# A hybrid decoder step on one core: the attention probabilities turned and multiplied later in each projection step, and two low-part subtractions moved off the first gather of the experts

## The chip, the cores and the metric

The kernel runs on one NeuronCore of a Trainium2 chip. The time is the device time of one execution in microseconds (us), and of several executions the median. The engines are TensorE (PE in the profile, with the loading of weights as PEld), VectorE (DVE), ScalarE (ACT), GpSimd (POOL) and SyncE (SP, which here only issues transfers). They run their own instruction streams and wait for each other through semaphores.

## The reference

One inference step of a decoder with one layer, for 1024 prompt tokens and 8 sample tokens, model width 1024:

```
h   = rmsnorm(x, n1) * (1 + sc1) + sh1
rq, rk, rv, rg, sq, sk, sv, za, zb = split(h @ w_in)
retention (4 heads of 128, chunks of 128, decay per head) on rotated rq, rk and on rv
sliding-window attention (8 query heads of 64 on 2 key heads, window 128, a learned sink per head)
    s = q k^T / 8 in the band;  m = max(max s, sink);  p = exp(s - m) / (sum exp(s - m) + exp(sink - m));  o = p v
merged = sigmoid(za) * (o_ret * silu(rg) @ w_up_ret) + sigmoid(zb) * (o_swa @ w_up_swa)
x   = x + g1 * (merged @ w_o)
h2  = rmsnorm(x, n2) * (1 + sc2) + sh2
experts: best group of 4, best 2 of its 8 experts, w2(silu(h2 w1) * (h2 w3)) weighted
y   = rmsnorm(x + g2 * experts, final_g)
```

The factors sh, sc and g come from silu(c) @ w_ada + b_ada, with w_ada of 1024 x 6144. Everything is in float32. Large products are done in three passes with each factor split into a high part (rounded to the matmul's float32r) and a low part (the rest): hi*hi + hi*lo + lo*hi.

## The kernel before

The tokens are 8 tiles of 128 prompt tokens and one of 8 sample tokens. The program is written out by hand, one stream for each engine, and the order of each stream is that in which its calls stand in the code. A step that stands earlier in one stream runs only when its semaphores allow, and holds all behind it.

**Projection steps.** `STEPS` has 36 entries (h, t): for each of four heads, tiles 0 to 8 (8 is the sample tile). The pass m of the loop (m from 0 to 36) works on three of them at once, PE in this order: parts 0 and 1 of the projection of `STEPS[m]` (`project_h`, L1700, 12 products of 512 columns), the turning of the rotated q and k of step m-1 (`turn_qk`, L1742), the turning of the probabilities of step m-2 into bank p5 (`turn_probs`, L1767), part 2, the product of the turned probabilities with V (`window`, L1778, into columns 256 to 383 of bank p7), the scores of step m-1 (L1747, L1751), part 3, and the output products of step m-1 (`outputs`, L1759 to L1761, into columns 0 to 255 of p7). In eight of the passes (`ADA_AT`: two per head) PE also does one part of the later modulation in bank p6 (`ada_later`, L1805), between the turning of the probabilities and part 2.

DVE goes, in pass m, through the rotation for step m-1 (L1099 to L1157), the normalising of the probabilities of step m-2 (L1187 to L1189), the copy out of the window's product (`window_out`, L1200), the softmax preparation of step m-1 (`weigh`, L1171 to L1183), in the eight passes the addition of the bias to the modulation (L1233, signals mod_r), and the copies out of p7 (`retention_out`, L1194 and L1195, signals st_u). ACT copies v and a scaled k, then the turned q and k (L770), then the turned probabilities (`probs_out`, L781, signals pT_e), squares the outputs (L785) and does the exponentials of step m-1 (L775). In the pass in which PE projects a sample tile, ACT also rounds the next head's weights in four parts (`head_round`, L738) and DVE subtracts to get their low parts (`head_rest`, L1088); parts 1 to 3 of the rounding stand behind the copy of the probabilities. Behind t = 2 of the later heads DVE normalises the outputs of the head before.

**From routing to the experts.** Behind the output projection each tile gets its second norm (DVE L1393, L1394), is turned and copied (ACT L899), gets router logits (PE L1977, DVE L1398), and DVE works out the expert and place of each token. When DVE has written the slots (L1508, L1509), POOL gathers the rows of the first three experts' tokens from DRAM (`gather_block`, L648), PE turns them (L2032), ACT and DVE split them, and PE multiplies them with the first expert's weights. These are split as well: ACT rounds each half (`half13`, L926 for the first expert, L941 later; each signals w13_hi) and DVE subtracts (`rest13`, L1512, in place, 128 x 2048; each signals w13_lo). For the first expert ACT's two halves stand behind the copy of the last tile, and DVE's two subtractions between the slots for the gather and those for the scatter.

## Time and profile before

| | us |
|---|---|
| median of 3 runs | 1367.56 |
| lowest and highest | 1364.56, 1368.78 |
| profiled execution | 1362.71 |
| its span, first to last instruction | 1360.9 |
| PE busy | 1223.7 (90%) |
| DVE busy | 747.4 (55%) |
| ACT busy | 509.0 (37%) |
| POOL busy | 172.8 (13%) |
| mean granted clock of PE, share of full speed | 0.959 |

The span is cut into stages by what PE does: first norm and keys and values to 98 us, projection steps to 442, gates and merge to 816, output projection and routing to 968, experts from 977 to 1304, and the weighted sum with the final norm to the end. Matmuls are pipelined, and one that starts behind a busy PE is shown from the point at which it begins to run to its modelled end, so two neighbours may overlap; the distance from one start to the next is then the better measure. A row that says xN stands for N instructions in a row. A number in brackets at a row's end is the time for which the engine had nothing to do ahead of it, and what ended it; "issue" there is time for which the profile shows no reason.

### The profile page before, as it was taken

To read this page: it belongs to the slowest core of one execution; us is meant where nothing else is said; L and a number is where in the kernel's file an instruction comes from. 1 tells how busy PE (TensorE), PEld (TensorE's weight loads), DVE (VectorE), ACT (ScalarE), POOL (GpSimd) and SP (SyncE) were. 2 spreads that over 40 slices of the span, in tenths; PEclk is the share of its full clock that TensorE was granted. 3 is DMA by queue.
4 is the path that set the end of the run, shared out by engine and by line. 5 is a ranking of instruction groups with operands and counts; after the bars stand their busy time and mean duration, and the time that the engine had idled before them with its cause. 6 is when DMAs were issued, how large, how long until landed. Compare 5 with 4: busy or idle time off the path is not lost.

```text
span 1360.9 us, 18012 instructions
## 1 busy us (share of the span) xinstructions
PE 1223.7 (90%) x6849; PEld 937.9 (69%) x6849; DVE 747.4 (55%) x1437; ACT 509.0 (37%) x862; POOL 172.8 (13%) x169
## 2 busy tenths in 40 slices
PE   4789999999998999999999998998499999988966
PEld 1677667667675788888888886886367666666732
DVE  0766565656566443111222206447599888887937
ACT  1643323323333221100111103111288878777832
POOL 2110000000000000000000001110222354444101
PEclk8799999999999999999999998999599999999988
DMA  9533222322222032111111005234589999999754
GB/s 359 196 141 111 89 80 88 131 101 80 88 83 82 28 123 114 47 47 47 47 46 44 2 0 188 78 136 179 182 299 371 373 353 367 358 354 357 291 222 179
DMA packets 40718, 219.75 MB, mean 161 GB/s; under 512 B 7432, under 2 KB 15056, under 8 KB 27978
## 3 DMA queue, kind: packets, MB, share of 16 engines
q1 hardware_dynamic: 32194, 197.15, 38.8%
q0 software_dynamic: 7536, 18.51, 4.0%
q10 hardware_dynamic: 928, 3.28, 0.7%
q8 instruction: 38, 0.62, 0.2%
q14 instruction: 22, 0.18, 0.0%
HBM read 202.03 MB, written 24.72 MB: 167 GB/s over the span
## 4 chain that ended last, share of the span: by engine, by line
PE 64%; DVE 16%; DMA 12%; issue 3%; ACT 3%; SPq 0%; POOL 0%; POOLq 0%; DVEq 0%; ACTq 0%
PE p L1934 10%; PE p L2042 8%; DMA G<-in_we 8%; PE p L1700 8%; PE p L1938 6%; PE psS L1961 4%; PE p L1870 3%; PE psS L1934 3%; PE p L1961 3%; PE psS L2061 3%; PE psS L1938 2%; PE p L1778 1%; DVE work L1189 1%; PE p L1767 1%; PE psS L1751 1%
## 5 line engine op out<-in xcount | busy, mean ns | idle before, releaser
L1700 PE MATMUL p<-A 128*128 128x512 f32 (+3 forms) x1080 | 259.0, 387 | 9.8 <-DVE A L1082 9.8
L1700 PEld LDWEIGHTS p<-A 128*128 128x128 f32 (+1 forms) x1080 | 175.7, 184 | 61.7 <-issue 12.7
L2042 PE MATMUL p<-C 128*96 128x512 f32 x768 | 194.0, 404 | 21.0 <-DVE C L1587 21.0
L2042 PEld LDWEIGHTS p<-C 128*96 128x96 f32 x768 | 122.0, 165 | 78.2 <-issue 31.1
L1512 DVE TENSOR_TENSOR C<-G,C 128x2048 fp32r<-128x2048 f32 x64 | 146.2, 2286 | 35.5 <-ACT C L941 35.5
L1341 DVE TENSOR_TENSOR work<-p,work 128x384 f32<-128x384 f32 (+1 forms) x36 | 18.6, 516 | 238.0 <-ACT work L871 237.6
L1934 PE MATMUL p<-A,B 128*128 128x384 f32 (+1 forms) x864 | 142.7, 323 | 2.0 <-DVE M L1274 2.0
L1934 PEld LDWEIGHTS p<-A,B 128*128 128x128 f32 x864 | 136.9, 188 | 4.5 <-issue 2.2
L941 ACT CAST C<-G 128x2048 fp32r<-128x2048 f32 x62 | 118.8, 1916 | 26.0 <-DMA G<-in_we 21.2
L2061 PE MATMUL psS<-C 128*96 128x512 f32 x384 | 95.9, 398 | 1.9 <-DVE C L1599 1.9
L655 POOL DMA_INDIRECT y_dram<-M,slotY x32 | 76.4, 2388 | 106.2 <-ACT M L975 106.2
L1938 PE MATMUL p<-M 128*128 128x384 f32 (+1 forms) x288 | 87.2, 452 | 0.0
L775 ACT ACTIVATE work<-work,small 128x256 f32<-128x256 f32 x64 | 32.1, 503 | 136.3 <-DVE small L1183 135.7
L2061 PEld LDWEIGHTS psS<-C 128*96 128x96 f32 x384 | 59.6, 162 | 24.7 <-DVE C L1581 2.1
L1576 DVE TENSOR_TENSOR C<-G,C 128x2048 fp32r<-128x2048 f32 x31 | 70.9, 2288 | 9.0 <-ACT C L947 8.8
L1938 PEld LDWEIGHTS p<-M 128*128 128x128 f32 x288 | 53.8, 190 | 23.9
L871 ACT ACTIVATE work<-p 128x384 f32<-128x384 f32 (+1 forms) x36 | 15.1, 455 | 133.4 <-PE psS L1938 133.4
L1961 PE MATMUL psS<-B 128*128 128x512 f32 (+1 forms) x240 | 59.5, 405 | 5.4 <-DVE B L1371 5.4
L648 POOL DMA_INDIRECT M<-h_dram,slotT x32 | 47.2, 1475 | 127.6 <-PE p L2032 106.7
L1200 DVE COPY M<-p 128x128 f32<-128x128 f32 x32 | 9.3, 291 | 96.1 <-PE p L1778 96.1
L947 ACT CAST C<-G 128x2048 fp32r<-128x2048 f32 x31 | 59.3, 1914 | 0.0
L626 POOL CAST B<-F 128x1024 fp32r (+2 forms) x8 | 8.9, 1112 | 396.5 <-DVE F L1347 331.1
(284 smaller groups left out, 1811.7 us busy)
## 6 DMA issues: line engine op xcount, KB each, us to landing
G<-in_we SPq DMA_DIRECT2D x32, 2048.0 KB, 18.0
G<-in_we SPq DMA_DIRECT2D x32, 1024.0 KB, 18.9
M<-in_w_ada SPq DMA_DIRECT2D x8, 2048.0 KB, 8.0
M<-in_x SPq DMA_DIRECT2D x18, 512.0 KB, 4.7
M<-in_rope SPq DMA_DIRECT2D x45, 192.0 KB, 2.4
D<-in_w_qkv SPq DMA_DIRECT2D x4, 2048.0 KB, 8.9
F<-in_lift SPq DMA_DIRECT2D x8, 1024.0 KB, 5.0
M<-y_dram SPq DMA_DIRECT2D x8, 1024.0 KB, 11.9
```

The lines of the kernel that those rows point to most:

```text
L648: pool.indirect_dma_start(out=xg[0:CAP, slot], out_offset=None, in_=h2_dram, in_offset=bass.IndirectOffsetOnAxis(ap=slotT[:, b:b + 1], axi ...
L655: pool.indirect_dma_start(out=y_dram, in_=yb[0:CAP, slot], in_offset=None, out_offset=bass.IndirectOffsetOnAxis(ap=slotY[:, b:b + 1], axis=0),
L941: nc.scalar.copy(half(h13, u), half(we[slot], u)).then_inc(s["w13_hi"], 1)
L947: nc.scalar.copy(h2w, we[slot][:, 4096:6144]).then_inc(s["w2_hi"], 1)
L1512: nc.vector.tensor_tensor(half(we_lo[slot], u), half(we[slot], u), half(h13, u), ALU.subtract).then_inc(s["w13_lo"], 1)
L1576: nc.vector.tensor_tensor(we_lo[slot][:, 4096:6144], we[slot][:, 4096:6144], h2w, ALU.subtract).then_inc(s["w2_lo"], 1)
L1700: last = mm(out, x[k][:, t0:t0 + rows], y(k), start=k == 0 and j == 0, stop=k == KD - 1 and j == 2)
L1934: mm(bs[j][:, 0:w0], w[slot][:, wc], x[:, cols], start=k == 0 and n == 0, stop=k == KD - 1 and n == 2)
L1938: last = mm(bs[2 + j][:, 0:w0], wy[slot][:, (4 * j + k) * P:(4 * j + k + 1) * P], src[:, k, cols], start=k == 0, stop=k == H - 1)
L1961: last = mm(o_bank[slot][n][0:rows], m[slot][:, k, 0:rows], w[k][:, cols], start=k == 0 and j == 0, stop=k == KD - 1 and j == 2)
L2042: last = mm(up_bank[slot][0:CAP, :], x[:, k, :], kcols(w, k), start=k == 0 and j == 0, stop=k == KD - 1 and j == 2)
L2061: last = mm(psS[0:CAP, nn, :], h[:, f, :], w[:, c0:c0 + 512], start=f == 0 and j == 0, stop=f == 1 and j == 2)
```

## The change

On PE, the turning of the probabilities moves from ahead of part 2 to behind it, and the product with V from ahead of the scores to behind part 3; its result goes into bank p6 and not p7. The modulation keeps its place ahead of part 2 and first waits for st_u of step m-2. As it uses p6 as well, in its passes PE waits for mod_r ahead of the product with V. On DVE, `window_out` moves behind `weigh` and the modulation's addition, and reads p6. ACT's order in the steps is as before.

At the experts' start, ACT's two roundings of the first expert's weights move ahead of the copy of the last tile; DVE's first subtraction moves ahead of the last tile's logits, and the second behind the slots for the scatter and the counts.

```diff
@@ ACT
+            half13(0)
+            half13(1)
             h2T_out(NT, NS)
             act.wait_ge(s["h2_r"], NT + 1)
             table(G2, 5, P)
-            half13(0)
-            half13(1)
@@ DVE, projection steps
-                nc.vector.tensor_copy(oswT[:, h, i * P:(i + 1) * P], p7[:, 256:384])
+                nc.vector.tensor_copy(oswT[:, h, i * P:(i + 1) * P], p6[:, 256:384])
...
-                    window_out(NT * h2 + t2_, h2, t2_)
                 if conv:
                     head_rest(conv, 1)
                 if t < NT:
                     weigh(n, h)
-                if conv:
-                    head_rest(conv, 2)
                 if m in ADA_AT:
...
+                if m >= 2 and STEPS[m - 2][1] < NT:
+                    window_out(NT * h2 + t2_, h2, t2_)
+                if conv:
+                    head_rest(conv, 2)
                 if t < NT:
                     retention_out(n, h, t)
@@ DVE, routing
             norm2(NT, NS)
+            rest13(0, 0, 0)
             logits(NT, NS)
...
-            rest13(0, 0, 0)
-            rest13(0, 1, 0)
             link(nc.vector.tensor_scalar(slot_y, s64[:, 0:NE], 2.0, float(2 * EMPTY), ALU.mult, ALU.add))
...
+            rest13(0, 1, 0)
+
             def expert(b, r):
@@ PE, window and projection steps
-                        last = mm(p7[r, 256:384], V_all[:, (i + b) * P + g * HD:(i + b) * P + (g + 1) * HD], prT[:, g, b, :],
+                        last = mm(p6[r, 256:384], V_all[:, (i + b) * P + g * HD:(i + b) * P + (g + 1) * HD], prT[:, g, b, :],
...
+                if m in ADA_AT:
+                    pe.wait_ge(s["st_u"], NT * prev2[0] + prev2[1] + 1)
+                    ada_later(ADA_AT[m])
+                if m < len(STEPS):
+                    project_h(m, 2)
                 if prev2:
...
                     turn_probs(NT * prev2[0] + prev2[1])
-                if m in ADA_AT:
-                    ada_later(ADA_AT[m])
-                if m < len(STEPS):
-                    project_h(m, 2)
-                if prev2:
-                    window(NT * prev2[0] + prev2[1], prev2[1])
                 if prev:
                     scores(NT * prev[0] + prev[1], prev[1])
                 if m < len(STEPS):
                     project_h(m, 3)
+                if m in ADA_AT:
+                    pe.wait_ge(s["mod_r"], ADA_AT[m] + 2)
+                if prev2:
+                    window(NT * prev2[0] + prev2[1], prev2[1])
                 if prev:
                     outputs(NT * prev[0] + prev[1], prev[0])
```

PE, the first pass with a part of the modulation (m = 2), before; L1805 is the modulation, L1767 the turning of the probabilities, L1778 their product with V:

```order
L1742 MATMUL p<-const,work 128x128 [waits rot]
L1742 MATMUL p<-const,work 128x128 x2
L1767 MATMUL p<-const,work 128x128 [waits pn_r,v_e,k_r]
L1767 MATMUL p<-const,work 128x128 x3
L1805 MATMUL p<-M,cT 32x128 [waits k_r,v_e,mod_r,ada_w]
L1805 MATMUL p<-M,cT 32x128 x31
L1700 MATMUL p<-A 128x512 x6
L1778 MATMUL p<-work,M 64x128 [waits v_e,st_u,pT_e]
L1778 MATMUL p<-work,M 64x128 x3
L1747 MATMUL p<-work 128x128 [waits qk_e]
```

And in the changed kernel, where the line numbers of this part are one higher (L1806, L1768, L1779):

```order
L1806 MATMUL p<-M,cT 32x128 [waits k_r,mod_r,v_e,ada_w,st_u]
L1806 MATMUL p<-M,cT 32x128 x31
L1701 MATMUL p<-A 128x512 x6
L1768 MATMUL p<-const,work 128x128 [waits pn_r,v_e,k_r]
L1768 MATMUL p<-const,work 128x128 x3
L1748 MATMUL p<-work 128x128 [waits qk_e]
L1752 MATMUL psS<-M,work 128x256 [waits kT_e]
L1752 MATMUL psS<-M,work 128x256
L1701 MATMUL p<-A 128x512 x6
L1779 MATMUL p<-work,M 64x128 [waits st_u,v_e,pT_e,mod_r]
L1779 MATMUL p<-work,M 64x128 x3
L1760 MATMUL p<-work 128x128 [waits at_r,kd_r,v_c]
```

The turning now has the six products of part 2 ahead of it, and the product with V the six of part 3 and, here, the wait for mod_r. In the other passes the same rows stand without the modulation and that wait.

DVE behind the slots for the gather, before; L1512 is the first expert's low parts, L1518 the slots for the scatter:

```order
L1509 TENSOR_SCALAR slotT<-work 96x29
L1512 TENSOR_TENSOR C<-G,C 128x2x1024 [waits w13_hi] x2
L1517 TENSOR_SCALAR work<-work 96x32
L1518 TENSOR_TENSOR slotY<-work 96x32 [waits dve_own]
L1521 COPY M<-p 128x32
```

And in the changed kernel, from the same instruction (L1515 there) to the first expert's tokens; the subtraction is L1476 there:

```order
L1515 TENSOR_SCALAR slotT<-work 96x29
L1516 TENSOR_SCALAR work<-work 96x32
L1517 TENSOR_TENSOR slotY<-work 96x32 [waits dve_own]
L1520 COPY M<-p 128x32
L1521 TENSOR_TENSOR work<-M,const 128x320 [waits dve_own]
L1523 TENSOR_REDUCE M<-work 128x32 [waits dve_own]
L1524 TENSOR_REDUCE M<-M 1x1 [waits dve_own]
L1525 CAST nover<-M 1x1 [waits dve_own]
L1476 TENSOR_TENSOR C<-G,C 128x2x1024 [waits w13_hi]
L1586 TENSOR_TENSOR C<-p,C 128x384 [waits xhi_r] x2
```

One of the two subtractions has gone up, ahead of the last logits, and the other stands behind seven small instructions.

## Rows read from the trace of the kernel before

**Rows 1.** PE's waits by cause: total us, times, longest, in the projection steps' lines.
```profile
PE p L1767 <- DVE work L1189: 10.3, 29, 2.7
...
PE p L1778 <- ACT work L781: 7.3, 4, 2.5
```
**Rows 2.** Timeline, a plain step on PE: start us, us, engine, line, count.
```profile
203.78 0.49 PE L1742 MATMUL p<-const,work 128*128 128x128 f32 x3
...
204.52 0.42 PEld L1767 LDWEIGHTS p<-const,work 128*128 128x128 f32 x4 [0.49 <-DVE work L1189]
204.52 0.66 PE L1767 MATMUL p<-const,work 128*128 128x128 f32 x4 [0.25 <-DVE work L1189]
...
204.93 1.64 PE L1700 MATMUL p<-A 128*128 128x512 f32 x6
...
206.50 0.66 PE L1778 MATMUL p<-work,M 128*64 128x128 f32 x8
...
207.09 0.49 PE L1747 MATMUL p<-work 128*128 128x128 f32 x2
...
208.15 1.65 PE L1700 MATMUL p<-A 128*128 128x512 f32 x6
...
209.63 0.38 PE L1759 MATMUL p<-work 128*128 128x128 f32 x2
```
**Rows 3.** Timeline, a step that turns no probabilities, on PE.
```profile
184.78 0.49 PE L1742 MATMUL p<-const,work 128*128 128x128 f32 x3
...
185.03 1.64 PE L1700 MATMUL p<-A 128*128 128x512 f32 x6
```
**Rows 4.** Timeline, a step with a part of the modulation, PE and DVE.
```profile
198.85 1.65 PE L1700 MATMUL p<-A 128*128 128x512 f32 x6
...
200.34 0.38 PE L1759 MATMUL p<-work 128*128 128x128 f32 x2
...
201.02 0.28 DVE L1233 TENSOR_TENSOR M<-p,M 128x128 f32<-128x128 f32 x1
```
**Rows 5.** Timeline, the two steps at the change from head 0.
```profile
168.43 1.05 ACT L738 CAST A<-D 128x1024 fp32r<-128x1024 f32 x1
...
170.16 1.21 DVE L1088 TENSOR_TENSOR A<-D,A 128x1024 fp32r<-128x1024 f32 x1
...
172.65 0.46 PE L1759 MATMUL p<-work 128*128 128x128 f32 x2 [0.21 <-DVE work L1176]
...
179.92 0.66 PE L1778 MATMUL p<-work,M 128*64 128x128 f32 x8 [1.59 <-ACT work L781]
```
**Rows 6.** Timeline, from the slots to the first gathered rows.
```profile
968.52 4.48 DVE L1512 TENSOR_TENSOR C<-G,C 128x2048 fp32r<-128x2048 f32 x2
...
969.53 4.51 POOL L648 DMA_INDIRECT M<-h_dram,slotT  x1 [20.26 <-DVE slotT L1509]
...
977.65 1.54 PE L2032 MATMUL p<-const,M 96*128 96x96 f32 x8 [9.58 <-DMA M<-h_dram,slotT]
```
**Rows 7.** Timeline, the last tile's logits, ACT and DVE.
```profile
952.93 0.19 ACT L899 COPY M<-p 128x32 f32<-128x32 f32 x1 [4.79 <-PE p L1970]
...
953.33 3.70 ACT L926 CAST C<-G 128x2048 fp32r<-128x2048 f32 x2
954.42 0.18 DVE L1398 TENSOR_TENSOR work<-p,brow 8x36 f32<-8x36 f32 x1 [2.60 <-PE p L1977]
```
**Rows 8.** Timeline, two later gathers and the subtractions beside them.
```profile
1006.73 2.28 DVE L1512 TENSOR_TENSOR C<-G,C 128x2048 fp32r<-128x2048 f32 x1
...
1008.58 1.29 POOL L648 DMA_INDIRECT M<-h_dram,slotT  x1 [4.12 <-PE p L2032]
...
1194.66 0.97 POOL L648 DMA_INDIRECT M<-h_dram,slotT  x1 [4.09 <-PE p L2032]
...
1195.01 2.29 DVE L1512 TENSOR_TENSOR C<-G,C 128x2048 fp32r<-128x2048 f32 x1 [2.27 <-ACT C L941]
```
**Rows 9.** Busy us (instructions), granted clock, DMA share, GB/s, end of the projection steps.
```profile
433.00:447.00 14.00, 8.53 (x43) 6.75 (x42) 11.48 (x37) 3.48 (x11) 1.86 (x2) 0.65 0.49 178
```

More of the change, by code:

```diff
@@ L919, in _ @@
             act.dma_start(FG, A["fg"].to_broadcast([P, D])).then_inc(s["tab_in"], 16)
-            h2T_out(NT, NS)
-            act.wait_ge(s["h2_r"], NT + 1)
-            table(G2, 5, P)
             def half13(u):
@@ L929, in _ @@
             half13(1)
+            h2T_out(NT, NS)
+            act.wait_ge(s["h2_r"], NT + 1)
+            table(G2, 5, P)
             act.wait_ge(s["gsh_r"], 3)
@@ L1472, in places, with rest13 @@
                     ALU.add, ALU.is_equal).then_inc(s["route_r"], 1)
+            def rest13(b, u, slot):
+                dve.wait_ge(s["w13_hi"], 2 * b + u + 1)
+                nc.vector.tensor_tensor(half(we_lo[slot], u), half(we[slot], u), half(h13, u), ALU.subtract
+                                        ).then_inc(s["w13_lo"], 1)
             merged_lo(NT, 0, NS)
@@ L1509, in _ @@
             nc.vector.tensor_scalar(slotT[:, 3:NE], s64[:, 3:NE], float(EMPTY), None, ALU.add).then_inc(s["route_r"], 1)
-            def rest13(b, u, slot):
-                dve.wait_ge(s["w13_hi"], 2 * b + u + 1)
-                nc.vector.tensor_tensor(half(we_lo[slot], u), half(we[slot], u), half(h13, u), ALU.subtract
-                                        ).then_inc(s["w13_lo"], 1)
-            rest13(0, 0, 0)
-            rest13(0, 1, 0)
             link(nc.vector.tensor_scalar(slot_y, s64[:, 0:NE], 2.0, float(2 * EMPTY), ALU.mult, ALU.add))
```

## The prediction

> **What bounds the kernel now.** I read the waits of TensorE (PE) first, then the timeline of one step of each kind, then the routing stretch, and last the POOL rows beside those of VectorE (DVE). The change touches two places that have nothing to do with each other.
>
> The first is the step phase, 98 to 442 us: 36 projection steps, four per eight token tiles and sample tile, and one closing pass. PE is the bound there. In the list of PE's waits [rows 1] stand 10.3 us in 29 waits for the turning of the probabilities (L1767, which waits for the normalising on DVE, L1189) and 7.3 us in 4 waits for their product with V (L1778, which waits for the copy on ScalarE, ACT, L781). In a plain step [rows 2] the reader sees that PE turns q and k at 203.78, can't go on, and starts L1767 at 204.52 with 0.25 us idle ahead; the third projection part comes at 204.93. In a step that turns no probabilities the third part follows 0.25 us behind the turning of q and k [rows 3]. Everything else in a plain step runs without a gap on PE. Rotation on DVE ends just as PE gets to the turning of q and k (behind a head's normalising it is late by 0.7 us), so that point has little slack; but it hangs on the output products, and what stands between these and the next turning is the same before and after.
>
> The second is the start of the experts. PE waits 9.58 us for the first gather [rows 6]. That gather takes POOL 4.51 us, where one that meets nothing takes 0.97 [rows 8], and DVE runs the two low-part subtractions of the first expert (L1512, 4.48 us) from just ahead of the first to its fourth microsecond.
>
> **The change, part by part.** *Plain steps.* Turning the probabilities moves behind the third part; the product with V moves from behind the third part to behind the fourth. Ahead of the third part go 204.93 - 203.78 = 1.15 us and 0.25 comes in their place: -0.90. Between the third part and the scores, L1767 now stands where L1778 stood; L1778 took 0.59 to the next instruction [rows 2], and L1767 with a waiting one behind it should take about as much; the third part before it may save some 0.05: call it -0.03. Behind the fourth part, 208.15 to 209.63 (1.48 us) becomes 1.57 (as 204.93 to 206.50) plus 0.59: +0.68. Sum -0.25 us a step, which is the idle time on L1767's row again. There are 4 such steps a head, 16 in all: -4.0. A few wait longer, 0.41 to 0.45, three of them right behind the normalising of a head's outputs: by the sum in [rows 1], 10.3 - 2.7 (the closing one) over 28 is 0.27 each, and the few over 0.25 make another -0.9, most of it where rotation was late too. Bounds per step: nothing (an issue gap of weight loads takes the stall's place) and -0.49, if the weight load's own idle time were what counted and all of it went.
> What hides the moved waits: the normalising has the whole third part as cover (1.6 us), ACT's copy the scores and the fourth part (2.2 us against 0.6).
>
> *Steps with a part of the later modulation (ADA_AT, 8 of them).* The product with V now writes the bank that these steps use, so PE waits ahead of it for mod_r, which DVE's addition L1233 gives. DVE does that addition behind the softmax preparation, as before. In [rows 4] the fourth part starts at 198.85 and L1233 ends at 201.30, so the product can start at about 201.35: 2.50 us behind the start of the fourth part, not 1.57. With 0.60 behind it and 1.49 saved (198.85 to 200.34) that is +1.61 instead of +0.68; against it stand the 0.90 ahead of the third part and a few hundredths. About +0.65 a step, 8 steps: +5.2. Bounds: +0.3 (the addition slips ahead of its row) and +0.95 a step (nothing won in exchange). Behind the waiting product stand the three output products and the next step's projection, so nothing covers it. This wait takes back what the plain steps give.
>
> *Steps at the change of heads.* ACT's copy of the probabilities stands ahead of its rounding of the next head's weights, part 1 (L738). That copy can't start now until PE has gone through the third part and the turning, so L738 begins some 1.05 us later than 168.43, DVE's L1088 (170.16 before, held there by the old copy of the window) about 0.4 later, and with it the scores' mask and the output products, which came at 172.65 [rows 5]. Here the product with V is already behind PE, so the 0.4 is all that is lost. In the next step PE does the whole third and fourth part before it needs ACT's copy; before, it stood 1.59 us [rows 5]. ACT's copy, which ended just ahead of 179.92, comes 0.6 later (the 0.4, and 0.2 for the window's copy that now stands ahead on DVE), so the product starts near 180.55 and the next head's projection 0.6 behind it, at 181.15. Before, the fourth part, 1.5 us, still stood between: 179.92 + 0.60 + 1.5 = 182.0. That is -0.87 a head, three heads: -2.6. Bounds 0 and -1.6 a head. At the fourth there is no projection left to put between: the 0.6 us by which DVE is late there stays, +0.6.
>
> Step phase: -4.0 - 0.9 + 5.2 - 2.6 + 0.6 = -1.7 us.
>
> *Low parts off the first gather.* Where the gathers overlap a DVE subtraction with both inputs in SBUF, they end a fixed time behind it: the one of 1008.58 ends at 1009.87, and L1512 ended at 1009.01, 0.86 before [rows 8]. The first ends at 974.04, 1.04 behind L1512's end at 973.00 [rows 6]. The gather of 1194.66 got in 0.35 us ahead of an L1512 and took 0.97 [rows 8]. So a gather is held at its beginning only. In the changed kernel DVE does seven small instructions behind the slots (1.9 us) and only then the second subtraction; a gather that starts at 969.53 is long past its beginning. It should end near 970.5: -3.5 us. The second gather may now be held by that subtraction, which costs nothing, as PE turns its rows ten microseconds later. The first subtraction goes into DVE's gap of 2.60 us ahead of the last logits at 954.42, 2.29 us into it (1006.73 is one of its kind); the two roundings on ACT (3.70 us for both) move ahead of the copies of 952.93, into 4.79 us in which ACT had nothing [rows 7]: they end by 952.0. They cost nothing, with 0.3 and 0.9 us to spare; if the cover were gone, a few tenths. What follows the gather (turning, tokens, the first expert, and the weight transfers that its end releases) is a chain, so the gain is kept through the expert stage. Bounds: 0 and -4.2.
> The Trainium skill, SBUF — State Buffer, section Who interferes with whom, says that a tensor_tensor with both inputs in SBUF holds GpSimd only where that reads SBUF, and infers that writing descriptors is not held by it. By that inference the subtractions would not be the cause and the sum would lack its 3.5 us. The rows disagree, unless it is the reading of the slots that is held, which the held beginning would fit.
>
> Sum: -1.7 - 3.5 = -5.2 us. The profiled execution took 1362.71 us (span 1360.9 and 1.8 around it), so it would come to 1357.5; it is 4.85 us faster than the median of the runs. From the median: 1367.56 - 5.2, about 1362.4 us.
>
> **The rivals.** *A: the first gather is slow because it is the first.* For it: no other gather in the profile is the first, and the subtractions hide nothing else. Against it: its end hangs on L1512's end as that of 1008.58 does [rows 6, 8]. Then only -1.7 is left: 1365.9 us.
> *B: the weight loads' idle time counts.* L1767's weight load stands idle 0.49 us, the product 0.25 [rows 2]. If all 24 plain and modulation steps win 0.24 more, and the heads too, it is -5.2 - 6.7: 1355.7 us. Against it: the step without probabilities, put together from [rows 3], gives 9.06 us and not 8.8.
> *C: the new wait lowers PE's clock.* Behind the two long waits at 438 and 441 us, 2.7 and 2.5 us, the granted clock of the stretch is 0.65 on average, so it fell to 1.2 GHz [rows 9]. If an idle 0.9 us in each of the eight steps did that too, at some 2 us a time, it would be +16 and the time 1378, slower. It decides from three such steps on. Against it: behind the 1.59 us of [rows 5] the eight products take the same 0.66 us as in a plain step.
>
> **How the numbers follow.** The main case 0.55, A 0.18, B 0.13, C 0.05; 0.09 is left for smaller mixtures, such as an expert stage that gives some of the gather's 3.5 us back to its weight transfers. The range: 1356.5 (most of B) to 1368 (A with modulation steps at their upper bound, +2.4, and little from the heads). A change over 0.3%, 4.1 us, is about what a measurement of this kernel can tell. The main case's 5.2 us is beyond it only by 1.1, so of its 0.55 some 0.40 counts as faster and 0.15 as the same. With B 0.13 and 0.03 of the rest: faster 0.56. A, 0.15 and most of the rest: same 0.37. C and a little: slower 0.07.
>
> **What would show it.** In the profile after: no PE wait on the turning of the probabilities but the closing one; 8 waits of 0.8 to 0.9 us on the product with V for the modulation's addition; the plain step 9.05 us from one turning to the next instead of 9.3; the step with modulation longer by 0.65; a first gather of about 1 us and the wait for it near 6 us. The prediction is wrong if the first gather stays at 4 us or more, if the plain steps shorten by 0.4, if the product's wait for mod_r isn't there, or if the expert stage from the first gathered rows to its end is longer than before by more than 2 us.

## The result and the profile after

| | before | after |
|---|---|---|
| median (runs), us | 1366.41 (4) | 1356.11 (4) |
| lowest and highest | 1364.56, 1368.78 | 1354.35, 1357.87 |
| profiled execution | 1362.71 | 1356.54 |
| its span | 1360.9 | 1354.6 |

The ratio of after to before over the runs is 0.9927, 95% interval 0.9909 to 0.9944. The medians differ by 10.3 us, where 5.2 were forecast, and 1356.11 lies just below the range, 1356.5 to 1368. In the two traces the span differs by 6.3 us. Cut into stages (start of the first turning of q and k, first gate product, start of the output projection, first gathered rows on PE, last expert, end) they show where it lies:

| stage, us | before | after | difference |
|---|---|---|---|
| to the first turning of q and k | 98.8 | 101.5 | +2.7 |
| projection steps | 343.9 | 337.1 | -6.8 |
| gates and merge | 378.9 | 379.3 | +0.4 |
| output projection, routing, first gather | 156.1 | 152.3 | -3.8 |
| experts | 337.0 | 338.0 | +1.0 |
| weighted sum and final norm | 46.2 | 46.4 | +0.2 |

The stages that the change touches, the second and the fourth, give -10.6. The first stage has no changed instruction and took between 97.9 and 102.2 us in the thirteen traces of this study; the experts took 336.9 to 338.6 in the kernels with the same code there. So a span from one trace is uncertain by some us, and the stages are what can be compared. The profiled execution of before, 1362.71, is also one of the shortest: 46 timed runs of it lie between 1362.66 and 1373.37.

The windows of the step phase, before and then after. Columns: stretch; its length, then busy us (instructions) of PE, PE's weight loads, DVE, ACT and POOL; granted clock, DMA share, GB/s.

```profile
98.80:442.69 343.89, 323.22 (x2206) 234.12 (x2204) 207.22 (x687) 116.74 (x371) 6.23 (x8) 0.99 0.27 96
```
```profile
101.50:438.60 337.10, 316.45 (x2205) 233.87 (x2203) 209.91 (x687) 116.18 (x371) 6.20 (x8) 0.99 0.28 99
```

The same instructions in less time, at the same clock: what is gone is gaps, and part of what the profile counts as busy.

PE's waits after, in the step phase:

```profile
PE p L1779 <- DVE M L1229: 6.7, 8, 0.8
PE p L1760 <- DVE work L1175: 4.6, 4, 1.2
PE p L1779 <- ACT work L781: 4.3, 4, 2.7
PE p L1768 <- DVE work L1188: 2.9, 1, 2.9
PE p L1743 <- DVE work L1156: 2.1, 3, 0.7
```

Against [rows 1], 28 of the 29 waits for the normalising are gone, and only the closing one stands (2.9 us). In their place are eight waits of 0.84 us on the product with V for the modulation's addition, and four of 1.16 on the output products, at the changes of heads.

A plain step after, on PE, answers to [rows 2]:

```profile
223.88 0.49 PE L1743 MATMUL p<-const,work 128*128 128x128 f32 x3
224.12 1.63 PE L1701 MATMUL p<-A 128*128 128x512 f32 x6
225.60 0.60 PE L1768 MATMUL p<-const,work 128*128 128x128 f32 x4
226.03 0.39 PE L1748 MATMUL p<-work 128*128 128x128 f32 x2
226.35 0.70 PE L1752 MATMUL psS<-M,work 64*128 64x256 f32 x4
226.98 1.67 PE L1701 MATMUL p<-A 128*128 128x512 f32 x6
```

and its weight loads from the fourth part on:

```profile
226.98 1.24 PEld L1701 LDWEIGHTS p<-A 128*128 128x128 f32 x6 [0.33 <-issue]
228.58 0.42 PEld L1779 LDWEIGHTS p<-work,M 128*64 128x64 f32 x8 [0.36 <-issue]
229.18 0.30 PEld L1760 LDWEIGHTS p<-work 128*128 128x128 f32 x2 [0.17 <-issue]
```

The third part follows the turning of q and k by 0.24 us, and no row has a wait. A step with modulation answers to [rows 4]; the reader sees the new wait on its product with V:

```profile
198.55 1.67 PE L1701 MATMUL p<-A 128*128 128x512 f32 x6
201.06 0.42 PEld L1779 LDWEIGHTS p<-work,M 128*64 128x64 f32 x8 [1.28 <-DVE M L1229]
201.06 0.67 PE L1779 MATMUL p<-work,M 128*64 128x128 f32 x8 [0.84 <-DVE M L1229]
201.66 0.49 PE L1760 MATMUL p<-work 128*128 128x128 f32 x2
```

The steps by kind, us from the start of one step's first output product to that of the next (L1759 before, L1760 after):

| kind of step | before | after | difference | forecast |
|---|---|---|---|---|
| plain (13) | 9.30 to 9.57 | 8.85 to 8.88 | -0.42 to -0.70 | -0.25 |
| behind a head's normalising (3) | 10.47 | 9.79 | -0.67 | more than -0.25 |
| with modulation (8) | 11.38 to 11.46 | 11.74 to 11.87 | +0.28 to +0.49 | +0.65 |
| last step of a head (4) | 9.57 | 9.96 | +0.39 | +0.4 |
| step behind it (3) | 16.33 | 15.14 | -1.2 | -0.87 with the row above |

The start of the experts answers to [rows 6]:

```profile
965.64 1.17 POOL L648 DMA_INDIRECT M<-h_dram,slotT  x1 [20.27 <-DVE slotY L1517]
...
966.48 2.27 DVE L1476 TENSOR_TENSOR C<-G,C 128x2048 fp32r<-128x2048 f32 x1
967.11 2.49 POOL L648 DMA_INDIRECT M<-h_dram,slotT  x1 [0.30 <-issue]
...
970.15 1.54 PE L2036 MATMUL p<-const,M 96*128 96x96 f32 x8 [5.97 <-DMA M<-h_dram,slotT]
```

The first gather takes 1.17 us and not 4.51. The second, which starts inside the subtraction, is the one held now: it ends at 969.60, 0.85 behind the subtraction's end.

### The profile page after: what moved, and what is told of

Same layout as the page of the kernel before. It is cut to its first block, busy times and chain, and to the rows that moved or that the text cites. A ratio compares the mean times of both kernels' runs of the same rounds, so it can differ in the third digit from the quotient of the medians.

```text
span 1354.6 us, 18020 instructions
## 1 busy us (share of the span) xinstructions
PE 1221.6 (90%) x6849; PEld 941.0 (69%) x6849; DVE 749.8 (55%) x1437; ACT 508.0 (38%) x862; POOL 180.6 (13%) x169
## 4 chain that ended last, share of the span: by engine, by line
PE 70%; DMA 12%; DVE 11%; ACT 3%; issue 3%; SPq 0%; POOL 0%; POOLq 0%; DVEq 0%; ACTq 0%
PE p L1701 13%; PE p L1938 10%; PE p L2046 9%; DMA G<-in_we 8%; PE p L1942 6%; PE psS L1965 4%; PE p L1874 3%; PE psS L1938 3%; PE psS L2065 3%; PE p L1965 3%; PE psS L1942 2%; PE p L1779 1%; PE psS L1752 1%; DVE C L1476 1%; PE p L1806 1%
## 5 line engine op out<-in xcount | busy, mean ns | idle before, releaser
L1701 PE MATMUL p<-A 128*128 128x512 f32 (+3 forms) x1080 | 260.6, 389 | 10.3 <-DVE A L1081 10.3
L1476 DVE TENSOR_TENSOR C<-G,C 128x2048 fp32r<-128x2048 f32 x64 | 146.1, 2284 | 35.0 <-ACT C L940 35.0
L655 POOL DMA_INDIRECT y_dram<-M,slotY x32 | 81.1, 2536 | 95.3 <-ACT M L974 95.3
L648 POOL DMA_INDIRECT M<-h_dram,slotT x32 | 50.8, 1587 | 127.8 <-PE p L2036 106.9
L871 ACT ACTIVATE work<-p 128x384 f32<-128x384 f32 (+1 forms) x36 | 15.1, 454 | 133.4 <-PE psS L1942 133.4
L1965 PEld LDWEIGHTS psS<-B 128*128 128x128 f32 (+1 forms) x240 | 41.5, 176 | 19.6 <-issue 5.8
```

The costliest lines, as they stand in the source:

```text
L648: pool.indirect_dma_start(out=xg[0:CAP, slot], out_offset=None, in_=h2_dram, in_offset=bass.IndirectOffsetOnAxis(ap=slotT[:, b:b + 1], axi ...
L655: pool.indirect_dma_start(out=y_dram, in_=yb[0:CAP, slot], in_offset=None, out_offset=bass.IndirectOffsetOnAxis(ap=slotY[:, b:b + 1], axis=0),
L1476: nc.vector.tensor_tensor(half(we_lo[slot], u), half(we[slot], u), half(h13, u), ALU.subtract).then_inc(s["w13_lo"], 1)
L1701: last = mm(out, x[k][:, t0:t0 + rows], y(k), start=k == 0 and j == 0, stop=k == KD - 1 and j == 2)
L1965: last = mm(o_bank[slot][n][0:rows], m[slot][:, k, 0:rows], w[k][:, cols], start=k == 0 and j == 0, stop=k == KD - 1 and j == 2)
```

## The experiments

All but those that say otherwise are edits of the changed kernel. Each group of runs was compared with runs of the kernel before on the same chip (medians 1365.59, 1366.67 and 1365.68 us; the run with half the products against a single one, 1364.11). A ratio is that of a run to the kernel before, with its 95% interval.

### The steps alone, and the experts' start alone

The experts' start put back as before (ACT's `half13` behind the last tile's copy, both of DVE's `rest13(0, ...)` behind the slots):

```diff
+            h2T_out(NT, NS)
+            act.wait_ge(s["h2_r"], NT + 1)
+            table(G2, 5, P)
             half13(0)
             half13(1)
-            h2T_out(NT, NS)
-            act.wait_ge(s["h2_r"], NT + 1)
-            table(G2, 5, P)
...
-            rest13(0, 0, 0)
             logits(NT, NS)
...
             nc.vector.tensor_scalar(slotT[:, 3:NE], s64[:, 3:NE], float(EMPTY), None, ALU.add).then_inc(s["route_r"], 1)
+            rest13(0, 0, 0)
+            rest13(0, 1, 0)
...
-            rest13(0, 1, 0)
```

> The changed kernel with the experts' start as before: only the projection steps are changed. Theory L (a stall costs what stands on the weight load's row, so the steps carry most of the gain, 6.8 us): 1359.8 us, a first gather of 4.5 us again and 9.6 us of waiting for it. Rival P (the steps are worth the 1.7 us that the prediction gave them, and the rest of the gain came from elsewhere, the expert stage say): 1364.7 us. The plain step is 8.88 us by L, and its length doesn't depend on the gather.

The other run is the kernel before with only the experts' start of the changed one.

> The kernel before with only the experts' start changed (roundings and low parts moved). Theory L: 3.5 to 3.8 us less than before, 1362.7 us, first gather 1.0 to 1.2 us long, the second held by the low part to about 2.5. Rival P: the gather's change brings the larger share, 8 us, 1358 us. If the expert stage gave the time back to its weight transfers it would be 1366.

Measured: the steps alone 1359.49 us, ratio 0.9961 (0.9948 to 0.9974), their stage 337.2; the experts' start alone 1363.77 us, ratio 0.9981 (0.9969 to 0.9993), steps 343.8, the stretch to the first gathered rows 152.4 and not 156.1. In the first, the gather is held again:

```profile
962.22 4.51 POOL L648 DMA_INDIRECT M<-h_dram,slotT  x1 [20.27 <-DVE slotT L1515]
...
970.16 1.54 PE L2036 MATMUL p<-const,M 96*128 96x96 f32 x8 [9.40 <-DMA M<-h_dram,slotT]
```

Against the medians, the parts are worth 6.1 us and 1.8, by the ratios 5.3 and 2.6; the product of the two ratios, 0.9942, lies within the interval of the whole. By the stages they are 6.7 and 3.7. The steps gave more than the 1.7 that the prediction had for them, but not the 8.4 of its rival B, which let the heads win too.

### Only the turning put back

```diff
+                if prev2:
+                    if m == 2:
+                        pe.wait_ge(s["k_r"], NT + 1)
+                        pe.wait_ge(s["v_e"], NT + 1)
+                    turn_probs(NT * prev2[0] + prev2[1])
                 if m in ADA_AT:
                     pe.wait_ge(s["st_u"], NT * prev2[0] + prev2[1] + 1)
                     ada_later(ADA_AT[m])
                 if m < len(STEPS):
                     project_h(m, 2)
-                if prev2:
...
-                    turn_probs(NT * prev2[0] + prev2[1])
```

> The changed kernel with only the turning of the probabilities put back ahead of the modulation and part 2; the product with V stays behind part 3. Theory L: the wait on the turning comes back in 28 steps, 0.25 us on the product's row and 0.49 on the load's, and costs 0.42 to 0.49 each, about +12.5 us: 1368. Rival P (it costs what stands on the product's row): 0.25 each, +7: 1363. If the late product with V alone gave the gain: 1356.

Measured: 1362.69 us, ratio 0.9970 (0.9953 to 0.9986); steps stage 345.2, 8.1 more than in the changed kernel. The price of the stall stands in 24 plain and modulation steps: +0.44 to +0.53 each, +0.67 behind a head's normalising. Two such stalls, first the products' rows, then the weight loads':

```profile
206.22 0.49 PE L1743 MATMUL p<-const,work 128*128 128x128 f32 x3
206.96 0.66 PE L1768 MATMUL p<-const,work 128*128 128x128 f32 x4 [0.25 <-DVE work L1188]
...
217.41 0.66 PE L1768 MATMUL p<-const,work 128*128 128x128 f32 x4 [0.45 <-DVE work L1188]
```
```profile
205.99 0.48 PEld L1743 LDWEIGHTS p<-const,work 128*128 128x128 f32 x3
206.96 0.42 PEld L1768 LDWEIGHTS p<-const,work 128*128 128x128 f32 x4 [0.49 <-DVE work L1188]
...
217.41 0.42 PEld L1768 LDWEIGHTS p<-const,work 128*128 128x128 f32 x4 [0.69 <-DVE work L1188]
```

The stall costs what stands on the weight load's row: 0.49 there and 0.46 in the step, 0.69 there and 0.67 in the step. The product's row has 0.25 and 0.45. In the flow a load starts ahead of its product (205.99 against 206.22), behind a stall both start together, and the product's row counts that lead as busy. The steps at the changes of heads went the other way, -0.76 and -0.15 each, since ACT gets on with the next head's weights sooner and PE's waits of 1.16 us are gone; over the four changes that is 3.5 us. So the stage grew by 8.1 and not by the 12.5 of theory L, and the time, 1362.69, is the one that rival P had named (1363). That is luck: the steps themselves show 0.46 and 0.67 and not the 0.25 that rival P took.

### DVE's addition ahead of the softmax preparation

```diff
-                if t < NT:
-                    weigh(n, h)
                 if m in ADA_AT:
                     i = ADA_AT[m]
...
                     nc.vector.tensor_tensor(mod2, p6[:, 0:P], mod2, ALU.add).then_inc(s["mod_r"], 1)
+                if t < NT:
+                    weigh(n, h)
```

> The changed kernel, but VectorE adds the bias to the modulation ahead of the softmax preparation and not behind it, so mod_r comes long before the product with V. Theory L: the eight waits of 0.84 us on PE go, each worth 0.9 us (the load's idle time beyond its usual 0.36): -7.3, about 1349 us. Rival R (the wait covers something, so that PE waits for the copy of the probabilities or the mask in its place): less than 2 us gained, 1354 or more.

Measured: 1352.19 us, ratio 0.9897 (0.9877 to 0.9917); steps stage 330.0, 7.1 less. Each of the eight steps is shorter by 0.91 (10.83 to 10.96 us), all others as they were. The stretch that waited before:

```profile
195.84 1.67 PE L1701 MATMUL p<-A 128*128 128x512 f32 x6
197.44 0.67 PE L1779 MATMUL p<-work,M 128*64 128x128 f32 x8
198.03 0.49 PE L1760 MATMUL p<-work 128*128 128x128 f32 x2
```

The fourth part to the product is 1.60 us, as in a plain step, where it was 2.51. So the new wait was all that kept these steps from the plain steps' gain, and one order on DVE removes it. The time shows less of it than the stage: 13.4 us below the kernel before, where the changed kernel is 10.3 below, 3.1 apart and not the 7.3 of theory L. The intervals of the two ratios overlap, so the gain of this edit alone rests on the trace; with the two further edits below, time and stage agree again.

### The product with V behind the output products

```diff
+                if prev:
+                    outputs(NT * prev[0] + prev[1], prev[0])
                 if m in ADA_AT:
                     pe.wait_ge(s["mod_r"], ADA_AT[m] + 2)
                 if prev2:
                     window(NT * prev2[0] + prev2[1], prev2[1])
-                if prev:
-                    outputs(NT * prev[0] + prev[1], prev[0])
```

and on DVE `window_out` behind `retention_out`.

> The changed kernel, but the product with V goes behind the output products, and VectorE's copy of it behind the retention copies. Theory L: mod_r is there by then (-7), rotation gets 0.6 us more time behind the normalising of a head (three waits of 0.7 shrink to 0.1, -1.8), and at the four changes of heads the product no longer fits into PE's wait for the mask (+2.4): -6.4, about 1349.7 us. Rival R: the copy of the window now stands ahead of the rotation, which has no slack, and makes every one of 28 steps wait 0.2 us (+5.6): 1355 us.

Measured: 1351.95 us, ratio 0.9894 (0.9879 to 0.9908), just below the changed kernel's interval and as good as the run before it, 1352.19 on the same chip. But the span of its profiled execution is 1353.6, against 1347.9 there: in the trace the steps stage is 335.4, only 1.7 less than in the changed kernel, and gates and merge take 1.8 more. The runs speak for a gain that the trace doesn't show. The profiled execution was the slowest of the four (1355.53 us) and had the lowest mean granted clock, 0.951 against 0.954 to 0.959 in the others; whether that is all of it stays open. The modulation steps are shorter by 1.6 and 0.9, but the last step of a head is 0.6 longer and the one behind it 1.7. At the change from head 0 PE waits 1.76 us, and then runs slower:

```profile
171.59 0.46 PE L1760 MATMUL p<-work 128*128 128x128 f32 x2 [1.76 <-DVE work L1175]
...
173.40 5.60 PE L1701 MATMUL p<-A 128*128 128x512 f32 x18
```

The window of those 18 products, in this run and then in the changed kernel:

```profile
173.40:178.84 5.44, 5.44 (x21) 4.34 (x20) 4.74 (x15) 0.70 (x4) 0.00 (x0) 0.76 0.00 0
```
```profile
175.42:179.67 4.25, 4.25 (x21) 3.42 (x20) 4.15 (x12) 1.19 (x5) 0.00 (x0) 1.00 0.00 0
```

The granted clock was 0.76 on average, so it fell to 1.2 GHz for a part of that stretch, and the same products took 1.19 us more. The 5.4 us behind the two other changes show 0.73 and 0.70. The changed kernel, with a wait of 1.16 us at the same place, shows 1.00.

### The product with V at full width, and at half its number

Two products with 128 columns of V as weights in place of four with 64 (half of the output is left out), and then two of the four as they are:

```diff
-                for g in range(2):
-                    r = slice(g * HD, (g + 1) * HD)
-                    for b in range(2):
-                        last = mm(p6[r, 256:384], V_all[:, (i + b) * P + g * HD:(i + b) * P + (g + 1) * HD], prT[:, g, b, :],
-                                  start=b == 0, stop=b == 1)
+                for b in range(2):
+                    last = mm(p6[:, 256:384], V_all[:, (i + b) * P:(i + b + 1) * P], prT[:, 0, b, :],
+                              start=b == 0, stop=b == 1)
```

> The changed kernel, but the window's product is two products over all 128 columns of V (first query head of the pair only, all into 128 partitions) in place of four over 64 columns each: the attention output of half the heads is wrong and half is left out. Its weight loads take the same 0.42 us by their rows (4 records of 128x128 in place of 8 of 128x64). Theory W (the idle time at either side of the product with V, 0.36 ahead and 0.17 behind on the load's row, comes with the change to a 64-wide tile and back): both go, 0.4 to 0.5 us less in each of 32 steps, about -14 us: 1342. Rival S (it comes with the semaphore waits of the product and of the one behind): nothing changes beyond a few hundredths: 1355.

```diff
-                for g in range(2):
+                for g in range(1 if n else 2):
```

> The changed kernel with only the first of the two 64-wide column groups of the product with V, from the second step on: two products of 64 columns of weights in place of four. Half of the window's output is left out. The run with two full-width products had as many, and took 0.35 us off each plain step. Theory W (what it took off was the change to a 64-wide part of the array and back, 0.36 + 0.17 us of idle loads): the gaps stay, since these products are still 64 wide, and the plain step stays within 0.1 of 8.88. Theory C (it was the number of products): the plain step falls by about 0.3, to 8.55, and the time to about 1348.

Measured: at full width 1347.5 us, ratio 0.9866 (0.9832 to 0.9899), plain steps 8.51 to 8.54 (-0.35). At half the number, a single execution: 1352.29 us, steps stage 336.8 against 337.1, plain steps 8.84 to 8.88, as in the changed kernel. The weight loads of both, and for the first the products behind them:

```profile
220.67 1.24 PEld L1701 LDWEIGHTS p<-A 128*128 128x128 f32 x6 [0.33 <-issue]
221.94 0.65 PEld L1777 LDWEIGHTS p<-work,M 128*128 128x128 f32 x4
222.18 0.61 PE L1777 MATMUL p<-work,M 128*128 128x128 f32 x4
222.51 0.30 PEld L1760 LDWEIGHTS p<-work 128*128 128x128 f32 x2
222.62 0.39 PE L1760 MATMUL p<-work 128*128 128x128 f32 x2
```
```profile
223.31 1.24 PEld L1701 LDWEIGHTS p<-A 128*128 128x128 f32 x6 [0.33 <-issue]
224.91 0.41 PEld L1779 LDWEIGHTS p<-work,M 128*64 128x64 f32 x4 [0.36 <-issue]
225.49 0.30 PEld L1760 LDWEIGHTS p<-work 128*128 128x128 f32 x2 [0.17 <-issue]
```

Theory W holds in its mechanism, and theories C and S fall: with half the products the step is as long, and the gaps of 0.36 and 0.17 us stay; at full width they are gone, with the semaphore waits where they were. From the product with V to the next instruction it is 0.44 us there (222.18 to 222.62) and 0.60 in the changed kernel; the turning, full width too, takes 0.43. In size theory W was too high. A step got 0.35 shorter and not 0.4 to 0.5, since the full-width loads take 0.65 us by their rows and not 0.42, and the steps with modulation, which still wait for mod_r, got 0.05 to 0.16. So the stage fell by 7.0 us (to 330.1) and not by 14. The two column groups run beside each other, so leaving one out saves nothing. What such a product costs in a stream of full-width ones comes with the gaps at its start and its end, 0.35 us a step here, and that price moved with it from the scores to the output products.

### What holds the gather

An extra reduction over 128 x 4096 with one input directly behind the slots, and, in the other run, the second subtraction directly behind the slots:

```diff
             nc.vector.tensor_scalar(slotT[:, 3:NE], s64[:, 3:NE], float(EMPTY), None, ALU.add).then_inc(s["route_r"], 1)
+            nc.vector.tensor_reduce(small[:, 40:41], R2[:, 0:4096], AX.X, ALU.max)
```

> The changed kernel with one more VectorE instruction behind the slots for the gather: a maximum over 128x4096 elements, one SBUF input, some 4.3 us, result unused. Theory D (a two-input VectorE instruction is what holds the gather): the first gather stays at 1.0 to 1.2 us although VectorE is busy for all of it. Rival E (any long VectorE instruction holds it): it takes 4 to 4.5 us and PE waits 9.5 us. Rival A (first gathers are slow by themselves) is out if it stays at 1.2.

```diff
             nc.vector.tensor_scalar(slotT[:, 3:NE], s64[:, 3:NE], float(EMPTY), None, ALU.add).then_inc(s["route_r"], 1)
+            rest13(0, 1, 0)
...
-            rest13(0, 1, 0)
```

> The changed kernel with the second low-part subtraction (2.28 us) directly behind the slots for the gather, where both stood before. Theory D: it is running when the gather comes, which then ends 0.85 to 1.05 us behind it: 2.2 to 2.4 us long in place of 1.17, and PE's first turning of tokens 1.2 us later. Rival A or E's opposite (nothing but the first subtraction mattered): 1.2 us long.

Measured, a single execution each: 1357.02 and 1357.12 us. The DVE and POOL rows, reduction first:

```profile
964.07 4.41 DVE L1516 TENSOR_REDUCE small<-M 128x1 f32<-128x4096 f32 x1
965.08 1.17 POOL L648 DMA_INDIRECT M<-h_dram,slotT  x1 [20.27 <-DVE slotT L1515]
966.55 0.97 POOL L648 DMA_INDIRECT M<-h_dram,slotT  x1 [0.30 <-issue]
```
```profile
965.49 2.28 DVE L1476 TENSOR_TENSOR C<-G,C 128x2048 fp32r<-128x2048 f32 x1
966.50 2.31 POOL L648 DMA_INDIRECT M<-h_dram,slotT  x1 [20.27 <-DVE slotT L1515]
```

DVE was busy for 4.41 us behind the slots in the first run, and two gathers passed beside it in 1.17 and 0.97. One subtraction of 2.28 us held the gather until 968.81, 1.04 behind its end, the same 1.04 as in [rows 6]. So it isn't that DVE is busy, nor that this gather is the first, but the subtraction. Of rival A only 0.20 us is left, by which the first gather is longer than the later ones when neither meets a subtraction (1.17 and 0.97). The later gathers agree: of the 32 in the trace of the kernel before, 22 started 0.08 us or more into a subtraction, and all but the first ended 0.83 to 0.88 us behind it, however long that made them (up to 3.05 us); two that started within 0.03 us of a subtraction's start took 0.96. That it is the two inputs in SBUF is not shown apart: the reduction also differs in writing only one column. One case speaks for it, with little margin: the gather of 980.06 started 0.32 us into a subtraction with one input in PSUM (0.56 us) and took 0.96, where held it would have taken 1.08.

### The change of heads

On top of the run with the addition ahead, the second part of the next head's low weights goes behind the softmax preparation on DVE:

```diff
-                if conv:
-                    head_rest(conv, 1)
...
                 if t < NT:
                     weigh(n, h)
+                if conv:
+                    head_rest(conv, 1)
```

> The run with the modulation's addition ahead of the softmax preparation, and one edit more: in the four steps at a change of heads DVE subtracts the second part of the next head's weights behind the softmax preparation and not ahead of it. In the changed kernel DVE has nothing to do for 2.1 us there (it waits for ACT's rounding, which stands behind the copy of the probabilities), the softmax preparation begins that much later, and PE waits 1.2 us for attT. Theory H (the step's 0.39 us over before, and most of the 1.09 over a plain step, is this wait): the step goes from 9.96 to about 8.9, but the subtractions behind it end only some 0.5 us sooner, so the next one (15.14) gets 0 to 0.6 back: steps stage 330.0 less 2 to 4, to 326 to 328, time about 1349. Theory N (the subtractions only move the wait to the product with V of the next step): stage within 0.5 of 330.0, time about 1352.

And on top of that, in the passes of a sample tile ACT's copy of the probabilities ahead of the copy of v (with a wait for srot on DVE ahead of the next head's first rotation, which keeps the order that the old place gave):

```diff
-                else:
-                    act.wait_ge(s["srot"], h + 1)
...
-                    nc.scalar.copy(vs[:, h, :], pj_bank[(m - 1) % 2][0:NS, 256:384]).then_inc(s["sv_c"], 1)
                 if m >= 2 and STEPS[m - 2][1] < NT:
                     h2, t2_ = STEPS[m - 2]
...
+                if t == NT:
+                    act.wait_ge(s["srot"], h + 1)
...
+                    nc.scalar.copy(vs[:, h, :], pj_bank[(m - 1) % 2][0:NS, 256:384]).then_inc(s["sv_c"], 1)
...
+                if n and n % NT == 0:
+                    dve.wait_ge(s["srot"], n // NT)
```

> The run before it (modulation's addition and the second subtraction moved) and one more edit: in the passes of a sample tile ACT copies the turned probabilities ahead of the sample tile's v, for which it waits until DVE's rotation has ended. In the changed kernel the product with V waits there 0.53 us for that copy in three of the passes and 2.9 us in the last. Theory H: these four waits go, 0.5 x 3 + 2.9 = 4.4 us, all of it if nothing else is late, so the time is about 1345. Theory M (the last pass has no projection behind it, and what follows waits for DVE's sample work all the same): only the three small ones, 1.5 us, time about 1347.5. If neither wait counted, the same as the run before it.

Measured: 1344.94 us, ratio 0.9842 (0.9820 to 0.9864), and 1340.25 us, ratio 0.9806 (0.9783 to 0.9829). The steps stages are 326.2 and 321.8. The last step of a head fell from 9.96 to 8.73; the one behind it rose from 15.14 to 15.42, where theory H had it 0 to 0.6 shorter, and then fell to 14.57. The second edit gave the 4.4 us of its theory H, but otherwise spread: three times 0.85 and 1.8 in the closing pass, where 0.5 and 2.9 were expected. The two rows that answer to the waits at the change of heads, with the first edit (and the weight load of the second) and then with both:

```profile
170.69 0.49 PE L1760 MATMUL p<-work 128*128 128x128 f32 x2
...
178.43 0.42 PEld L1779 LDWEIGHTS p<-work,M 128*64 128x64 f32 x8 [1.21 <-ACT work L781]
178.44 0.67 PE L1779 MATMUL p<-work,M 128*64 128x128 f32 x8 [0.78 <-ACT work L781]
```
```profile
168.83 0.49 PE L1762 MATMUL p<-work 128*128 128x128 f32 x2
...
175.73 0.67 PE L1781 MATMUL p<-work,M 128*64 128x128 f32 x8
```

Both waits are gone in the last run. PE's order is the same in both runs, so this is a clean price of a stall: 0.85 us in the step, 0.78 on the product's row, and 1.21 on the load's row, less the usual 0.36, which is 0.85. It is the best version, 25.4 us below the kernel before, where the changed one is 10.3 below: 15.1 us more, 15.3 by the steps stage, by the order of DVE's and ACT's work in the steps.

## Why the prediction was wrong

The steps it named are the ones that moved, each the way it said. It failed in one term, the size of a plain step, and that term is in 24 steps.

*Plain steps, forecast -0.25, measured -0.42 to -0.47 in most.* Put beside each other by starts on PE, before [rows 2] and after: ahead of the third part 1.15 and 0.24 (forecast and measured -0.9). From the third part to the scores 2.16 (1.57 + 0.59) and 1.91 (1.48 + 0.43), where the prediction let L1767 take about as much as L1778 and booked -0.03. Here is the failed step. The 0.59 of L1778 holds the gaps of a 64-wide product, which the experiment at full width shows (0.60 there became 0.44); the turning is full width and takes 0.43, and the third part ahead of it has no gap at its end either. Booking 0.59 in both places counted these gaps twice, and the term of -0.03 measured -0.25. Of the rest, the scores to the fourth part lost 0.11, fourth part and product gained 0.72 (forecast +0.68), and the stretch from the output products to the next turning came 0.11 longer. Sum -0.44. The prediction's own sign of being wrong, plain steps shorter by 0.4, is what came.

The same error in the other view: the prediction checked its sum against the idle time on the product's row, 0.25, and took the match for a proof. The weight load's row had 0.49, and the run with only the turning put back shows that this is the price. The upper bound of the term was right, and rival B with it, for these steps; its counter-argument, a step of 9.06 us put together from [rows 3], is 9.31 less the same 0.25, so it was no second witness. The few longer waits gave -0.67 each behind a normalising, not the 0.4 of the product's rows.

*Modulation steps, forecast +5.2, measured +3.2.* The wait for mod_r came as worked out (the product at 2.51 us behind the fourth part, forecast 2.50). The difference is again what the plain steps gained more than booked. The lower bound, the addition ahead of its row, didn't happen by itself; moved there by hand it was worth 7.1 us in the stage.

*Change of heads, forecast -2.6 and +0.6.* The last step of a head +0.39, as forecast. The one behind it gained 1.2, so a change is worth -0.8 and three -2.4. At the fourth head the 0.39 and some 0.2 in the closing pass make the +0.6. These terms were right.

*Steps together:* -1.7 forecast, -6.8 in the trace, 6.1 (of 1359.49 against 1365.59) in the run with the steps alone.

*First gather, forecast -3.5, measured -3.8* in its stage, and -1.8 in the medians of the run with it alone (2.6 by the ratio, whose interval reaches from 1.0 to 4.2 us). Rival A falls by both runs on the gather, but for 0.20 us. Whether a part of the gain is lost later can't be told: the experts' stage in that run's trace was 1.1 longer than in before's, but between kernels with the same experts' code it varied by 1.7. The Trainium skill, SBUF — State Buffer, Who interferes with whom, has a DVE instruction with two SBUF inputs contend with a GpSimd instruction that reads SBUF, and only infers that the writing of descriptors isn't held. The gather as a whole was held: 4.51 and 2.31 us with the subtraction, 1.17 without. Which part of it is held, its reading of the slots or its descriptors, no run tells apart, so the inference is neither borne out nor refuted; it was only no ground to price the gather at nothing. The same section's rule that a reduction never contends on trn2 agrees with 1.17 beside one of 4.41 us.

*Rival C.* The clock of the steps stayed at 0.99, as before, and was full behind the wait of 1.16 us. But the clock can fall so: behind 1.76 us, in the run with the product last, it fell to 1.2 GHz for some of the next products, and these took 1.2 us more. Behind the 1.59 us of [rows 5] it had not (1.00 from 179.92 to 184 us).

*The total.* It was counted from the median of three runs, 1367.56; with the fourth it is 1366.41, from which the forecast would have been 1361.2, 5.1 over the result. The sum over the touched stages, -10.6, and the difference of the medians, -10.3, agree, though the two parts by themselves came to 7.9 in the medians. Of the 5.4 us between -10.6 and -5.2, the 24 plain and modulation steps are 3.3 + 2.0.

## What to carry to other kernels

The price of a stall of PE stands on the weight load's row, less the gap that this load has without the stall: 0.49 against 0.46 measured, 0.69 against 0.67, 1.28 less 0.36 against 0.91, and 1.21 less 0.36 against 0.85. When an instruction group moves, its length goes with it only if its neighbours are of its kind; a product on half of the array's columns takes its gaps along, worth 0.35 us a step here, and a full-width one that takes its place doesn't have them. A new wait on a bank is often one place in another engine's order: the three edits of order on DVE and ACT here, each read off one wait, were worth 15 us, the change itself 10.

## What the runs showed of the hardware

- A stall of PE cost the idle time on the weight load's row less the load's usual gap: 0.46 us where that row had 0.49, 0.85 where it had 1.21 less 0.36.
- Four products of 64 columns of weights in two column groups took as long as two in one group: 0.60 us from the first load to the next instruction's with four, 0.58 with two.
- An indirect gather on POOL that starts while DVE subtracts with both inputs in SBUF ends 0.83 to 0.88 us behind the subtraction's end, the first one 1.04; one past its beginning when the subtraction starts, as the first gather after (0.84 us in, 1.17 us long), is not held; beside a reduction of 4.41 us the first gather took the same 1.17.
- Behind a wait of 1.76 us at each of three changes of heads PE's granted clock was 0.70 to 0.76 on average over a stretch of 5.4 us; behind waits of 1.16 us, in the changed kernel, and 1.59 us, in [rows 5], it was 1.00.
